# Weight block sums of the two down projections: from VectorE in the projections to GpSimd beside the first feed-forward

## The reference

```
h = rms_norm(x, norm_ffn)                                        # block 1
x = x + (silu(h @ w_ffn_gate) * (h @ w_ffn_up)) @ w_ffn_down     # inner width 2816
gate = sigmoid(rms_norm(x, norm_ple) @ w_ple_gate)
x = x + gate * (p @ w_ple_proj)
...
# block 2: up = causal_dwconv(h @ w_up, ...), split in gate and value,
#          y = (gelu(gate) * value) @ w_down, then norms and a residual
```

## Time and profile before

| | us |
|---|---|
| median of 3 runs | 2708.07 (2702.29 to 2712.51) |
| the profiled execution | 2705.71 |
| its span | 2703.9 |
| PE busy in the span | 2583.1 (96%) |
| DVE busy | 1786.3 (66%) |
| ACT busy | 1189.3 (44%) |
| POOL busy | 1199.0 (44%) |

### The profile page before, as it was taken

How to read it: one execution, slowest core, us unless ns; L and a number is a source line. 1 busy time by engine, 2 the same in 40 slices (tenths; PEclk the granted TensorE clock), 3 DMA queues, 4 the chain that set the end, 5 groups by cost and what they waited for, 6 DMA issues and landing times.

```text
span 2703.9 us, 32099 instructions
## 1 busy us (share of the span) xinstructions
PE 2583.1 (96%) x11826; PEld 2081.1 (77%) x11826; DVE 1786.3 (66%) x2176; ACT 1189.3 (44%) x2076; POOL 1199.0 (44%) x764
## 2 busy tenths in 40 slices
PE   7999999999899999999898999998999999999997
PEld 6887788888688888888676777877767777777875
DVE  6888876653855454589945556427378666666997
ACT  6777421122533333444454243355354444444444
POOL 2444522223455555556633311134433555554566
PEclk9999999999999999999999999999999999999998
DMA  3000044432122222565422112122321222226753
GB/s 123 24 24 24 19 149 155 153 113 109 47 79 85 86 78 94 170 232 176 144 78 89 48 31 46 32 76 69 132 86 63 78 86 71 86 78 221 253 177 132
DMA packets 119580, 271.59 MB, mean 100 GB/s; under 512 B 12664, under 2 KB 26232, under 8 KB 119296
## 3 DMA queue, kind: packets, MB, share of 16 engines
q1 hardware_dynamic: 119424, 269.54, 30.1%
HBM read 231.15 MB, written 38.34 MB: 100 GB/s over the span
## 4 chain that ended last, share of the span: by engine, by line
PE 56%; DVE 22%; ACT 6%; POOL 6%; DMA 5%; issue 5%; SPq 0%; DVEq 0%; ACTq 0%; POOLq 0%
PE psum_mem L750 20%; PE psum_mem L1045 15%; PE psum_mem L1075 4%; POOL w_lo L3958 3%; DVE tmp_mem L3672 3%; DMA w_raw<-in_w_up_b 2%; PE psum_mem L1244 2%; PE psum_mem L1249 2%; PE psum_mem L1246 2%; PE psum_mem L812 2%; DVE x_lo_a L3065 2%; DVE w_raw L2942 1%; PE psum_mem L796 1%; DVE w_raw L3048 1%; PE psum_mem L847 1%
## 5 line engine op out<-in xcount | busy, mean ns | idle before, releaser
L3958 POOL TENSOR_TENSOR w_lo<-w_raw,w_hi 128x512 fp32r<-128x512 f32 x320 | 495.9, 1555 | 464.2 <-ACT w_hi L1834 447.6
L3864 POOL TENSOR_TENSOR w_lo<-w_raw,w_hi 128x1024 fp32r<-128x1024 f32 (+2 forms) x105 | 237.4, 2261 | 624.5 <-ACT w_hi L1599 542.0
L1834 ACT CAST w_hi<-w_raw 128x512 fp32r<-128x512 f32 x320 | 196.4, 620 | 323.2 <-DMA w_raw<-in_w_up_b 72.1
L1045 PE MATMUL psum_mem<-h_hi,w_hi 128*128 128x512 f32 x672 | 266.4, 396 | 20.9 <-ACT norm_row L2470 18.2
L1045 PE MATMUL psum_mem<-h_lo,w_hi 128*128 128x512 f32 x672 | 264.0, 393 | 1.3 <-DVE h_lo L2951 1.3
L1045 PE MATMUL psum_mem<-h_hi,w_lo 128*128 128x512 f32 x672 | 263.2, 392 | 0.0
L750 PE MATMUL psum_mem<-h_hi,w_hi 128*128 128x512 f32 x736 | 232.1, 397 | 11.4 <-ACT h_hi L1633 8.9
L750 PE MATMUL psum_mem<-h_lo,w_hi 128*128 128x512 f32 x736 | 228.8, 392 | 5.7 <-DVE h_lo L3582 5.5
L750 PE MATMUL psum_mem<-h_hi,w_lo 128*128 128x512 f32 x736 | 228.3, 391 | 2.7 <-POOL w_lo L3864 2.7
L1599 ACT CAST w_hi<-w_raw 128x1024 fp32r<-128x1024 f32 (+2 forms) x105 | 100.3, 955 | 266.9 <-PE psum_mem L750 253.8
L750 PEld LDWEIGHTS psum_mem<-h_hi,w_hi 128*128 128x128 f32 x736 | 137.9, 189 | 43.4 <-ACT h_hi L1633 8.9
(11 more groups left out here) (466 smaller groups left out, 6434.1 us busy)
## 6 DMA issues: line engine op xcount, KB each, us to landing
hidden<-tmp_mem SPq DMA_DIRECT2D x44, 512.0 KB, 2.6
w_raw<-in_w_up_b SPq DMA_DIRECT2D x44, 512.0 KB, 3.7
w_raw<-in_w_ffn_down SPq DMA_DIRECT2D x77, 256.0 KB, 3.4
w_raw<-in_w_down_b SPq DMA_DIRECT2D x77, 256.0 KB, 3.2
x_ring_a<-hidden SPq DMA_DIRECT2D x66, 256.0 KB, 3.3
x_ring_b<-hidden SPq DMA_DIRECT2D x66, 256.0 KB, 3.2
w_raw<-in_w_in_a SPq DMA_DIRECT2D x32, 512.0 KB, 3.7
ada_raw<-in_w_ada SPq DMA_DIRECT2D x64, 256.0 KB, 3.3
```

The lines of the kernel that those rows point to most:

```text
L1045: made = e.matmul(out, wt, x, start=j <= DIFF_3 and k == 0 and part == 0, stop=k == KH - 1 and part == 2, skip_group_check=True)
L1834: e.copy(w_slot(w_hi, slot, of), source).then_inc(*S.of("w_hi", key))
L3864: e.tensor_tensor(w_lo[:, i, 0:width], w_raw[:, i, 0:width], w_hi[:, i, 0:width].bitcast(F32), ALU.subtract).then_inc(*S.of("w_lo", c))
L3958: e.tensor_tensor(w_slot(w_lo, slot, of), source, w_slot(w_hi, slot, of).bitcast(F32), ALU.subtract).then_inc(*S.of("w_lo", key))
```

## The change

The four weight sums of a down tile (M_5, M_7, M_6, M_3) are no longer made by DVE in the down projections. POOL makes them, for both projections (22 tiles, 11 of each), beside pairs 1 to 19 of the first feed-forward: `sum_tiles_beside(i)` gives one tile for each pair and two for pairs 1, 7 and 13. SP loads a tile's two rows of blocks (1 MB) to one of two buffers, POOL makes four 128x512 sums in place in a row, each waiting for the one before, behind the pair's DIFF_4 fill, and SP writes the tile (1 MB) to a new array in DRAM, `down_sums`, from which `w_load` then takes its blocks. `keep_w` and its 22 loads go. With it:

- both down projections go by the order M_1, M_2, M_5, M_6, M_7, M_4, M_3, so in block 1 the last product now goes to rows 0 to 3, second half of the tokens, and `ple_high`, `ple_square`, `ple_low` and the row sums go half by half, the first four already in the fourth product; the small `gains` move from the end to unit 15;
- in ACT's list the cast of `w_pp` (`ahead(1)`) now stands behind the last four `ple_row`;
- in block 2's pairs DVE's `back_sum` of the next pair goes between the two tap additions of the value half, and its `weight_high_sum` ahead of `ffn_product`;
- unit 3 of block 2's down projection is formed before GELU and the product of the last pair, and `hidden_out` of the last pair stands behind the load of unit 6 in SP's list, for both blocks.

The diff, cut to its core:

```diff
+W_SUM = {M_6: 0, M_7: 1, M_3: 2, M_5: 3}
+SUM_TILES = [(of, kt) for of in "ab" for kt in range(KF // 2)]
+def sum_tiles_beside(i):
+    return [n for n in range(len(SUM_TILES)) if 1 + n * 19 // len(SUM_TILES) == i]
...
             def down_sums(of, u):
-                if m in W_KEPT + W_MADE:
...
-                        e.tensor_tensor(kept, kept, raw, ALU.add).then_inc(*S.of("dn_sum", (of, "w", u)))
...
-                        e.tensor_tensor(raw, raw, kept, ALU.subtract).then_inc(*S.of("dn_sum", (of, "w", u)))
...
+            def first_tile_sums(n):
+                low, high, late, high_late = (sum_part(n, j) for j in range(4))
+                w.wait_ge(f"in_ws{n % 2}", (n, 1))
+                e.tensor_tensor(high_late, high, high_late, ALU.add).then_inc(*S.of("ws_sum", (n, M_5)))
+                w.own("ws_sum")
+                e.tensor_tensor(high, low, high, ALU.subtract).then_inc(*S.of("ws_sum", (n, M_7)))
...
             for _, i in FFN_PAIRS:
                 for j in (UP_HIGH, GATE_HIGH, DIFF_4):
                     fill_pair(i, j)
...
+                for n in sum_tiles_beside(i):
+                    first_tile_sums(n)
+                    last_tile_sums(n)
                 if i < KF - 1:
                     for j in (UP_LOW, SUM_2, DIFF_3, SUM_1):
                         fill_pair(i + 1, j)
...
+            for k in range(KH):
+                ple_row(k, 1)
             ahead(1)
-            for k in range(KH, KD):
-                w.wait_ge(*down_added("a", 6, k - KH))
-                ple_high(k, 0)
...
             for _, i in FFN_PAIRS[PLAIN:]:
-                back_sum(i)
-                weight_high_sum(i, "b")
...
-                whole_rest(i, 1, up_banks(i))
+                late_taps = tap_rest(i, 1, up_banks(i))
+                next(late_taps)
+                if i < KF - 1:
+                    back_sum(i + 1)
+                else:
+                    down_low("b", 3)
+                for _ in late_taps:
+                    pass
+                if i < KF - 1:
+                    weight_high_sum(i + 1, "b")
                 ffn_product(i)
...
+                for n in sum_tiles_beside(i - 1):
+                    sum_out(n)
+                for n in sum_tiles_beside(i):
+                    sum_load(n)
...
-            hidden_out("b", KF - 1)
             for u in range(4, DOWN_UNITS):
                 w_load("b", u)
+                if u == 6:
+                    hidden_out("b", KF - 1)
```

More of the change, by code:

```diff
@@ L1140, in tensor @@
                 if m == 0:
-                    w.wait_ge("row_v", ("ple", 7))
-                    w.wait_ge("row_g", ("ple", (7, 1)))
+                    for half in range(NH):
+                        w.wait_ge(*ple_added(half, KD - 1))
                     sum_partitions("ple", norm_row, (("inv_m", ("ple", 1)),))
@@ L3153, in vector, with last_row_add @@
-            for k in range(KH):
-                ple_low(k)
-            for k in range(KH, KD):
-                ple_low(k, 1)
+                elif p == 3 and kt in (1, 3, 5, 7):
+                    ple_low(kt // 2, 0)
+                elif p == 6 and 1 <= kt < 5:
+                    ple_low(KH + kt - 1, 1)
+                elif p == 6 and 7 <= kt:
+                    ple_low(KH + kt - 7, 0)
+            def last_row_add(at):
+                w.wait_ge("square", ("ple", (1, PLE_ROWS[1][at])))
+                w.wait_ge(*ple_added(1, at - 1))
+                ple_row_add(e, "row_v", 1, at)
```

266 lines of the change are left out of this document (145 added, 121 removed), and 3 rows, old and new, of the table SHARED.

## The result

The changed kernel takes 2735.35 us (median of 4 runs, 2735.1 to 2739.5), the kernel before 2708.47 (4 runs, 2702.29 to 2712.51). The ratio is 1.0105, with a 95% interval of 1.0083 to 1.0126: slower by 27 us, where 12 us less was forecast. The profiled execution has a span of 2733.3 us against 2703.9.

What follows compares the result with a forecast made beforehand. PE was taken as what nearly everything waits for, losing time to late engines. Gains -(8 + 1 + 17 + 15) = -41 against 24 + 5 = +29 gave -12 us: 2694 us, forecast's own range 2683 to 2705, overall range 2676 to 2712.

Steps and rivals of the forecast that it cites:

- First pairs, +29: First feed-forward's pairs: POOL's sums make PE wait; 24 us in three double pairs, 5 in the single ones.
- Rival 2: First pairs: DVE instructions wait for whole POOL sums or fills, DVE becomes the bound; +30, 2738 us; chance 0.06.
- (a): Block 1's down projection: without DVE's 44 weight sums its `x_lo` is in time; 8 us back, bounds 5.6 to 9.2.
- (b): Passage behind block 1's down projection: low parts earlier, cast of `w_pp` later; 1 us back, bounds 3 worse to 4 better.
- T: In (b), PE's end in block 1's down projection; `w_hi` from the `w_pp` cast was forecast at T + 5.0.
- (c): Block 2's pairs: earlier `back_sum` removes PE's wait on ACT's copy; 17 us back, bounds 5 to 20.
- Rival 3: Block 2's pairs: copy held by ACT's casts or raw loads late; (c) gives 2, not 17: +3, 2711; chance 0.11.
- (d): Block 2's down projection: changed orders give 6 us, DVE's sums and other waits gone 9; 15 back, bounds 8 to 18.

Runs made afterwards that it cites:

- e5: Changed kernel with POOL's 88 sums left out; tiles still loaded and stored, unsummed: 2706.6 us.
- e9: Changed kernel with half loads, `hidden_out` behind the raw loads, and VectorE's order of before in block 2's pairs: 2702.9 us.
- e6: Changed kernel with `hidden_out` behind the raw loads and row 0's raw load cut into halves in block 2's pairs: 2701.6 us.
- e15: Changed kernel with only the eight loads of `x_last` spread, one every third unit, in block 2's down projection: 2727.7 us.
- e8: Changed kernel with `x_last`'s loads spread and the first two weight loads of block 2's down projection put ahead of the last `hidden_out`: 2724.5 us.
- e11: Changed kernel with e6's and e8's edits and the double pairs' second tile summed one sum at a time in POOL's gaps: 2674.6 us.
- e12: e11 with the GATE_HIGH half's read and first tap ahead of the down projection's first casts and lows in block 2's last pair: 2675.2 us.
- e4: Changed kernel with a tile's four POOL sums split, two behind each of two fills, instead of in a row behind DIFF_4: 2811.3 us.
- e13: Kernel before with the half loads alone and `hidden_out` behind the raw loads in block 2's pairs, VectorE's old order kept: 2689.9 us.

## Why the prediction was wrong

*First pairs, +29: right.* +28.8, with the three waits of 6.77, 6.21 and 6.19 us where the double pairs are (6.4 forecast), and the clock behind each. At 751 to 757 the granted clock is 0.50 and 12 matmuls take the time of 26. The parts fit too: the double pairs cost 26 us (24 forecast), the others 0 to 0.3 us each (0.3 forecast). Rival 2 did not come, though its first half did: VectorE is busy 284.4 us instead of 213.2 with one instruction more, 228.2 with the transfers alone (e5). So some 56 us of length come from meetings with POOL; two instructions of the low sums with two inputs in SBUF (L2941, L2951) have means of 1.72 and 1.62 us, where the kernel before has 0.69 for both. They fell into time that VectorE had, since pairs with one tile are at most 0.3 us longer. The Trainium skill, SBUF — State Buffer, "Who interferes with whom", has the port pair that the two engines share as an exclusive lock, for which a VectorE instruction with two inputs in SBUF contends with GpSimd's reads. The lengths agree with that; what they cost was decided by VectorE's idle time. Rival 2's total, 2738 us, is near the 2735.4 measured, but by luck: it put 71 us into these pairs.

*(a) -8: right,* -8.5; PE waits 0.7 us on `x_lo` in the whole stage. VectorE is busy 179.9 us in it, though, more than the 165 that the prediction gave as a sign; it had room all the same.

*(b) -1: nearly right,* +0.8 in the passage itself. PE waited 4.4 us for the cast of `w_pp`, which came at T + 4.6 (T + 5.0 forecast); the mean clock of the 21 us behind is 0.76, where 0.91 stood before.

*(c) -17: the step that failed.* It came out at +13. The step was: "The wait on the copy goes, 15.2 us, and with it the slow matmuls behind every stop: 17 of 21.6." The wait did go. But it was not what the pair's length hung on. The loop of a pair closes through the raw weight slot: weight_high_sum, DIFF_4's cast and `w_lo`, the second raw load, UP_LOW's cast and `w_lo`, and the low sums on VectorE. The four corners, in the kernel before and in the changed one, show that the raw load is in it (us from the first form to the down projection; "half loads" stands for these with `hidden_out` behind the raw loads):

```
                     whole loads   half loads
before,  old order      406.2        388.2
before,  new order      419.6        385.3
changed, old order      402.5        388.3
changed, new order      419.5        385.1
```

The half loads give 14 to 18 us in the old order and 34 in the new; the new order alone costs 13 to 17; on top of the half loads it gives 3, all in the second pair of the stretch (23.5 us in e9, 20.2 in e6). In the kernel before the move of `hidden_out` was not run alone; there the store went out at 2260.18, 2.4 us ahead of the first raw load, and did not hold it back. The second failing sentence is the one that allowed for the cost: "so `hidden_out` and the pair's weight loads behind that in SP's list, by 1 to 2 us, for which ACT has room." The sizes were about right (2.8 and 0.9 us later against PE). The room was not there: ScalarE had idled 4.19 us before because it waited for that very load, and the lateness of the data, 2.4 us, went in full through cast and `w_lo`; PE's stops and the pair's 0.7 us are what was left of it. Rival 3 named this ("the raw loads come late") and was given 0.11 and 2711; like (c)'s bounds, 5 to 20, it excluded a loss.

*(d) -15: mechanism right, one collision missed.* It gave -3.5. DVE's sums went and its later waits on `x_lo` with them. But the loads behind the 4 MB burst of `x_last` now came late for VectorE, 10.21 us in the row above. The prediction never looked at that burst. It took 8 to 9 us (e15). With the load order as well (e8) the stage is 13 us shorter than before, close to the 15. In e8 a first stop of 1.2 us and one of 2.9 behind it stand in place of the old 3.5. In e11 the second is 1.6; e12 halved it, and the time stayed.

(c) and (d) are 30 and 12 us of the 41 by which the forecast was off. The tile transfers, costed at nothing, cost at most 2 us in the pairs.

## What to carry to other kernels

The engine that PE names in its last wait may be the place where a loop's length shows, not its cause: before pricing the removal of a wait, follow that engine's own list back to the first thing it waits for from outside. Here a row of 37 us, VectorE's wait on a transfer, stood in the trace of the kernel before. A wait of 40.9 us stood beside it and was harmless, so a row names a candidate, and a run that takes that wait alone away decides. When a step moves an instruction, ask of each transfer behind it whether its receiver already waits for it; if it does, that receiver's idle time is no room.

## What the runs showed of the hardware

- After PE's stops of 6.77, 6.21 and 6.19 us its matmuls came 0.43 us apart, not 0.23, for the next 4.9, 4.0 and 3.5 us (granted clock 0.50 at 751 to 757, 0.60 at 875 to 881, 0.69 at 999 to 1005). In e4, after single stops of 1.1 and 1.4 us (at 765.1, 749.9 and 872.3) they came 0.23 to 0.24 apart; after stops of 2.0 to 2.1 us they came 0.23 to 0.24 apart in some places (974.5, 1100.3) and 0.43 in others (826.7, 1123.4).
- The 512 KB raw load of block 2 lands after 3.7 us (median) in the kernel before and 4.9 in the changed one, where both loads and a 512 KB store go out within 1.3 us. Halves of 256 KB take 2.9 (e6, e13).
- A float32 sum of 128x512 on POOL took 1.28 to 1.30 us in 22 of the 88 of the changed kernel, and 1.59 to 1.75 in the other 66.
